# Interleaved high and low activation rows, at fixed offsets modulo 256 bytes, and a 256 / 288 split of the 544 columns

## The chip, the cores and the metric

The kernel runs on one core of a Trainium2 chip. The metric is the time of one execution on the device, in microseconds (us). A difference of about 0.2% is what a measurement of this kernel can tell from no change.

## What is computed

The reference is a two-layer streaming encoder for 512 prompt frames and 32 sample frames of width 1024: in every layer a SwiGLU feed-forward block (hidden size 2816), a recurrent mixer (Mamba-2 and gated linear attention heads in layer 0, HGRN2 heads in layer 1), and a second feed-forward block. Nearly all arithmetic is in dense products of 544 token columns with float32 weights:

```python
def swiglu(x, w_gu, w_down):
    gate, up = jnp.split(x @ w_gu, 2, axis=-1)
    return (jax.nn.silu(gate) * up) @ w_down

for l in range(DEPTH):
    h = h + 0.5 * swiglu(rms_norm(h, p['norm_ffn1'][l]), p['ffn1_w_gu'][l], p['ffn1_w_down'][l])
    u = rms_norm(h, p['norm_mix'][l])
    ...
    h = h + m
    h = h + 0.5 * swiglu(rms_norm(h, p['norm_ffn2'][l]), p['ffn2_w_gu'][l], p['ffn2_w_down'][l])
y = rms_norm(h, p['norm_final'])
```

## The kernel before

Activations lie transposed: 128 features on the partitions, the T = 544 tokens along the free dimension, one "row" of 544 float32 numbers (2176 bytes) for each of KT = 8 groups of 128 features. Each float32 operand is split into a high part (rounded to the type float32r, which TensorE multiplies in one pass) and a low part (the remainder), and a product is made of three: high weight times high row, high weight times low row, low weight times high row.

There are two kinds of dense work on TensorE.

- Plain rows (`row_products`, L2500 to L2516). A unit is one block of 128 output features; it runs over k = 8 (or 6, 4, 7) input rows r and adds all into one line of the PSUM tensor PD. The 544 columns don't fit one PSUM bank of 512, so each product is cut at FRONT = 288 into a front of 288 columns and a rest of 256. One row is six matmuls of 128x128 weights, each with its own weight load.
- Products of the feed-forward up-projections (`product`, L2605 to L2619), a 2x2 block scheme with seven products p1 to p7 for a hidden tile. Each is 4 rows q of three matmuls (L2617, L2618, L2619) with 272 columns, half of T. Products 1, 2, 3 and 7 read XB, 4, 5 and 6 read XT. p1 and p2 start at column 0 of a row, p3 and p7 at column 272.

The moving operands (what streams through TensorE) are these SBUF tensors: XB (the normed input of a block, 8 rows high and 8 rows low), AB (the gated hidden values, rows of the down-projections), YB, GOB and COB (mixer outputs) and XT (sums for the products). In all but XT the eight high rows stand first and the eight low rows behind them, `[2, KT, T]`; x[:, 0, r, :] in `row_products` is the high row r, x[:, 1, r, :] the low one.

Where these tensors start follows from `place`, which lays one after the other, rounded up to 64 bytes. The byte addresses in a partition are: XB 18560, AB and COB 98304, YB and GOB 102528, XT 190464. The weights of plain rows stand in whi and wlo (69760 and on, a block of 512 bytes for each row, so all at 128 modulo 256), the weights of the products in WH and WL (from 133120, all at 0 modulo 256). KW holds the last unit's weights that were loaded early (133120).

The instruction order of each engine is written out by hand. ScalarE rounds weights (whi, L653) and writes high rows (XH L680, AH L763), VectorE makes the low weights (wlo, L1488) and low rows (XL L1526, AL L1658), SyncE issues the weight loads. TensorE waits for them through semaphores at the start of each unit (`lo_ready`, `pair_read`) and, in the first unit over a new operand, at each row.

Of the kernel before, what the change touches and what calls it, by code (L numbers as in the profile page):

```python
# [6 lines left out]
FR = mybir.dt.float32r  # L7
# [5 lines left out]
P = 128  # L13
D = 1024
KT = D // P
TP, TS = 512, 32
T = TP + TS
HT = T // 2
FRONT = 288
REST = T - FRONT  # L20


# [8 lines left out]
KR = 8  # L31
# [18 lines left out]
WHOLE = 3  # L50
# [38 lines left out]
def build(nc, a, o):  # L89
# [3 lines left out]
    with ExitStack() as ctx:  # L93
# [3 lines left out]
        def at(name, shape, offset, dt=F):  # L97
            return nc.alloc_sbuf_tensor_at(name, [P] + list(shape), dt, offset=offset)

        def place(name, shape, where, dt=F):  # L100

            off, n = where[0], 4
            for s in shape:
                n *= s
            where[0] += (n + 63) // 64 * 64
            assert where[0] <= nc.sbuf_usable_end, (name, where[0], nc.sbuf_usable_end)
            return at(name, shape, off, dt)


        w = [(nc.sbuf_base + 63) // 64 * 64]  # L110
        H = place("H", [KT, T], w)
        XB = place("XB", [2, KT, T], w, FR)
        XH, XL = XB[:, 0], XB[:, 1]
        V = at("V", [2, 4, 4 * P], w[0])
        raw = [place(f"raw{s}", [KR, P], w) for s in range(4)]
# [18 lines left out]
        free = w[0]  # L134


        w = [free]
# [5 lines left out]
        SQX = place("SQX", [D], w)  # L143
        WIDE = place("WIDE", [5, P], w)

        w = [free]
        AB = place("AB", [2, 8, T], w, FR)
        AH, AL = AB[:, 0], AB[:, 1]
        late = w[0] + 2 * 7 * 4 * P * 4 - 9 * HT * 4
        WH, WL, WS = {}, {}, {}  # L150
        for b in (1, 0):
# [1 line left out]
            WL[b] = place(f"WL{b}", [7, 4 * P], w, FR)  # L153
            WS[b] = at(f"WS{b}", [4, 4 * P], w[0] - 4 * 4 * P * 4)
        VF = at("VF", [4, 4 * P], late + 9 * HT * 4 - 2 * 7 * 4 * P * 4)
        KW = at("KW", [KT - WHOLE, 2, KR, P], free + 2 * 8 * T * 4, FR)
        assert free + (2 * 8 * T + (KT - WHOLE) * 2 * KR * P) * 4 <= w[0]
        xt_at = w[0]
        XT = place("XT", [2, 4, 3, HT], w, FR)
        tg_at = w[0]  # L160
# [6 lines left out]
        DH = at("DH", [HT], late)  # L167
        XN = at("XN", [HT], late + HT * 4)
        TF = at("TF", [3, HT], late + 2 * HT * 4)
        T3 = at("T3", [4, HT], free + 14 * T * 4)  # L170
        YF = at("YF", [2, T], tg_at)
        yout = at("yout", [NC + 1, D], xt_at)
        assert (NC + 1) * D <= 2 * 4 * 3 * HT
# [1 line left out]
        w = [free]  # L175
# [63 lines left out]
        w = [GM["end"]]  # L239
# [5 lines left out]
        w = [free]  # L245
# [9 lines left out]
        def high_of(u):  # L255

            return KW[:, u - end_unit - WHOLE, 0] if kept(u) else whi[u % 2]

# [11 lines left out]
        def line(b):  # L270

            at0 = 1024 * (b % 2) + 512 - FRONT
            return PDF[:, at0:at0 + T]
# [2225 lines left out]
        def _(pe):  # L2499
            mm = pe.matmul  # L2500

            def row_products(ps, r, x, first, final, before=None):

                out = line(ps)
                front, rest = out[:, 0:FRONT], out[:, FRONT:T]
                hi, lo = high_of(ps)[:, r, :], low_of(ps)[:, r, :]
                if before:
                    before(0)
                mm(front, hi, x[:, 0, r, 0:FRONT], start=first, stop=False)  # L2509
                mm(rest, hi, x[:, 0, r, FRONT:T], start=first, stop=False)  # L2510
                if before:
                    before(1)
                mm(rest, hi, x[:, 1, r, FRONT:T], start=False, stop=False)  # L2513
                mm(front, hi, x[:, 1, r, 0:FRONT], start=False, stop=False)  # L2514
# [89 lines left out]
            def product(s, p):  # L2604

                b, w, out = s % 2, W_OF[p], bank(s, BANK_OF[p])
                if p <= 3:
                    k0, t0 = ((0, 0), (4, 0), (4, HT))[p - 1]
                    moving = XB[:, :, k0:k0 + 4, t0:t0 + HT]
                elif p == 7:  # L2610
                    moving = XB[:, :, 0:4, HT:T]
                else:
# [58 lines left out]
            def ffn(f, e, final=False):  # L2671

                tag = FFNS[f][0]
                if f:
                    run(f"{tag}_up", XB, x_parts(e), lambda: mean_square(e), ORDER if f == 3 else None)
                else:
                    run_rest(f"{tag}_up", XB)
                    pe.wait_ge(S["rs_ready"], 1)
                    for n in range(2):
                        mm(PM[:, n, 0:HT], whi[0][:, 0, :], XH[:, 0, 0:HT], start=True, stop=True)  # L2680
                for g, nf, ss in groups(f):
# [10 lines left out]
                    for s in ss:  # L2692
# [8 lines left out]
                        else:  # L2701
                            unit_rows(u0, 0, 2, nf, AB, before)
                            p3(s)
# [95 lines left out]

            run("ab_small", XB, x_parts(1))  # L2800
            mean_square(1)
# [397 lines left out]
```

## Time and profile before

| | us |
|---|---|
| median of 3 runs | 2326.39 |
| lowest, highest | 2325.65, 2327.73 |
| span of the profiled execution | 2325.5 |

| engine | busy us | share of the span | instructions |
|---|---|---|---|
| PE (matmul) | 2294.0 | 99% | 20579 |
| PEld (weight load) | 2266.2 | 97% | 20579 |
| DVE | 1720.5 | 74% | 2587 |
| ACT | 1143.9 | 49% | 1769 |
| POOL | 14.4 | 1% | 50 |

Matmuls are pipelined: one takes 270 to 310 ns from its start to its end, but the next starts some 120 to 130 ns after it. So the busy time of a matmul is not its price; the price is the distance from its start to the start of the next, which the timeline shows. The timeline's starts are rounded to 0.01 us, so that the length of one row of six matmuls is known to 10 ns from one row, and to 1 or 2 ns from several rows in succession.

### The profile page before, as it was taken

What the parts mean: (1) busy time and instruction counts of PE and PEld (TensorE: products, weight loads), DVE (VectorE), ACT (ScalarE), POOL (GpSimd) and SP (SyncE); (2) the same over time, 40 slices, a digit from 0 to 9 for tenths busy, and PEclk for the clock granted to TensorE, in tenths of its full rate; (3) what the DMA queues carried; (4) which work ended last, traced back from release to release, by engine and by line L of the source; (5) the groups of instructions that cost most, each with busy time, mean ns of one, the idle gap of its engine ahead of it and who ended that gap; (6) DMA issues with size and microseconds to landing.
All of it is one profiled execution on the core that took longest, in us unless ns stands there. A gap on an engine that the chain in (4) does not pass through costs nothing.

```text
span 2325.5 us, 49874 instructions
## 1 busy us (share of the span) xinstructions
PE 2294.0 (99%) x20579; PEld 2266.2 (97%) x20579; DVE 1720.5 (74%) x2587; ACT 1143.9 (49%) x1769; POOL 14.4 (1%) x50
## 2 busy tenths in 40 slices
PE   8999999999999999999999999999999999999998
PEld 8999999999999999999999999999999999999998
DVE  7767876788577567677867767876888867767885
ACT  6434444676354545343445434444677756424453
POOL 1000000000000000000000000000000000000000
PEclk9999999999999999999999999999999999999999
DMA  4323333332422223333323323332222223323331
GB/s 149 105 77 103 94 96 86 94 119 74 121 71 63 76 82 93 98 92 106 95 82 98 111 75 103 95 94 84 70 71 68 69 74 91 96 82 102 88 107 57
DMA packets 397773, 209.92 MB, mean 90 GB/s; under 512 B 11679, under 2 KB 393750, under 8 KB 397558
## 3 DMA queue, kind: packets, MB, share of 16 engines
q1 hardware_dynamic: 392166, 203.17, 30.7%
q10 hardware_dynamic: 5392, 3.72, 0.5%
q8 instruction: 155, 2.54, 0.5%
q14 instruction: 60, 0.49, 0.1%
HBM read 201.41 MB, written 5.45 MB: 89 GB/s over the span
## 4 chain that ended last, share of the span: by engine, by line
PE 83%; DVE 7%; ACT 4%; DVEq 3%; issue 1%; ACTq 1%; DMA 0%; SPq 0%
PE PD L2509 8%; PE PM L2619 8%; PE PM L2617 8%; PE PD L2514 8%; PE PM L2618 8%; PE PD L2515 8%; PE PD L2513 7%; PE PD L2510 7%; PE PD L2516 7%; PE PD L2619 3%; PE PD L2617 3%; PE PD L2618 3%; DVE wlo L1488 1%; DVE c_xl L2199 1%; DVE c_xl L2175 1%
## 5 line engine op out<-in xcount | busy, mean ns | idle before, releaser
L653 ACT ACTIVATE whi<-raw 128x1024 fp32r<-128x1024 f32 (+3 forms) x231 | 229.1, 992 | 356.7 <-PE PD L2516 350.8
L1488 DVE TENSOR_TENSOR wlo<-raw,whi 128x1024 fp32r<-128x1024 f32 (+3 forms) x233 | 267.3, 1147 | 69.3 <-ACT whi L653 47.9
L2509 PE MATMUL PD<-XB,whi 128*128 128x288 f32 x856 | 262.8, 307 | 2.2 <-DVE wlo L1488 2.0
L2514 PE MATMUL PD<-XB,whi 128*128 128x288 f32 x856 | 252.8, 295 | 0.0
L2515 PE MATMUL PD<-XB,wlo 128*128 128x288 f32 x856 | 252.0, 294 | 0.0
L2513 PE MATMUL PD<-XB,whi 128*128 128x256 f32 x856 | 241.9, 283 | 0.3 <-DVE XB L1526 0.3
L2510 PE MATMUL PD<-XB,whi 128*128 128x256 f32 x856 | 240.0, 280 | 0.0
L2516 PE MATMUL PD<-XB,wlo 128*128 128x256 f32 x856 | 238.3, 278 | 0.0
L2619 PE MATMUL PM<-XT,WL 128*128 128x272 f32 x720 | 208.3, 289 | 0.0
L2617 PE MATMUL PM<-XT,WH 128*128 128x272 f32 x720 | 207.6, 288 | 0.0
L2619 PE MATMUL PM<-XB,WL 128*128 128x272 f32 x720 | 207.6, 288 | 0.0
L2617 PE MATMUL PM<-XB,WH 128*128 128x272 f32 x720 | 207.5, 288 | 0.0
L2618 PE MATMUL PM<-XT,WH 128*128 128x272 f32 x720 | 207.1, 288 | 0.0
L2618 PE MATMUL PM<-XB,WH 128*128 128x272 f32 x720 | 207.0, 287 | 0.0
L2509 PE MATMUL PD<-AB,whi 128*128 128x288 f32 x664 | 196.9, 297 | 0.0
L2514 PE MATMUL PD<-AB,whi 128*128 128x288 f32 x664 | 196.4, 296 | 0.0
L2515 PE MATMUL PD<-AB,wlo 128*128 128x288 f32 x664 | 194.6, 293 | 0.0
L2513 PE MATMUL PD<-AB,whi 128*128 128x256 f32 x664 | 188.7, 284 | 0.0
L2510 PE MATMUL PD<-AB,whi 128*128 128x256 f32 x664 | 186.4, 281 | 0.0
L2516 PE MATMUL PD<-AB,wlo 128*128 128x256 f32 x664 | 185.1, 279 | 0.0
L2509 PEld LDWEIGHTS PD<-XB,whi 128*128 128x128 f32 x856 | 161.1, 188 | 5.7 <-issue 2.8
L2515 PEld LDWEIGHTS PD<-XB,wlo 128*128 128x128 f32 x856 | 162.1, 189 | 0.0
(519 smaller groups left out, 6683.7 us busy)
## 6 DMA issues: line engine op xcount, KB each, us to landing
raw<-in_ffn_w_down SPq DMA_DIRECT2D x64, 512.0 KB, 3.8
V<-in_ffn_w_gu SPq DMA_DIRECT2D x60, 512.0 KB, 3.9
V<-in_ffn_w_gu SPq DMA_DIRECT2D x120, 256.0 KB, 4.5
raw<-in_ab_w_in SPq DMA_DIRECT2D x44, 512.0 KB, 3.9
raw<-in_ffn_w_gu SPq DMA_DIRECT2D x32, 512.0 KB, 3.8
raw<-in_c_w_in SPq DMA_DIRECT2D x32, 512.0 KB, 4.0
raw<-in_ffn_w_down SPq DMA_DIRECT2D x32, 384.0 KB, 3.3
VF<-in_ffn_w_gu SPq DMA_DIRECT2D x12, 512.0 KB, 4.6
```

Of the source, the lines that this page charges most:

```text
L653: A(high_of(ps)[:, 0:k, :], raw[ps % 4][:, 0:k, :], ACT.Copy).then_inc(S["hi_ready"], 1)
L1488: TT(low_of(u)[:, 0:k, :], raw[u % 4][:, 0:k, :], high_of(u)[:, 0:k, :].bitcast(F), ALU.subtract).then_inc(S["lo_ready"], 1)
L2175: TT(xn[:, :, 0, :], mid, bn[:, :, 0, :], ALU.subtract)
L2509: mm(front, hi, x[:, 0, r, 0:FRONT], start=first, stop=False)
L2510: mm(rest, hi, x[:, 0, r, FRONT:T], start=first, stop=False)
L2513: mm(rest, hi, x[:, 1, r, FRONT:T], start=False, stop=False)
L2514: mm(front, hi, x[:, 1, r, 0:FRONT], start=False, stop=False)
L2515: mm(front, lo, x[:, 0, r, 0:FRONT], start=False, stop=final)
L2516: return mm(rest, lo, x[:, 0, r, FRONT:T], start=False, stop=final)
L2617: mm(out, hi, moving[:, 0, q, :], start=q == 0 and opens, stop=False, skip_group_check=not opens)
L2618: mm(out, hi, moving[:, 1, q, :], start=False, stop=False, skip_group_check=not opens)
L2619: last = mm(out, lo, moving[:, 0, q, :], start=False, stop=q == 3, skip_group_check=not opens)
```

## The change

The split moves from 288 / 256 to 256 / 288 columns. XB and AB are laid out as `[KT, 2, T]`: the low row of r stands right behind the high row of r. `rearrange` gives all users the old index order, so no other line of XB or AB changes. AB starts 128 bytes later (98432), and 128 bytes are left free behind it, so WH, WL, XT and what follows move by 256 bytes and keep their offset modulo 256, while KW moves by 128. YB, GOB, COB and XT keep their layout.

```diff
@@ -16,7 +16,7 @@
-FRONT = 288
+FRONT = 256
@@ -109,7 +109,7 @@
-        XB = place("XB", [2, KT, T], w, FR)
+        XB = place("XB", [KT, 2, T], w, FR).rearrange("p k s t -> p s k t")
         XH, XL = XB[:, 0], XB[:, 1]
@@ -143,9 +143,11 @@
-        w = [free]
-        AB = place("AB", [2, 8, T], w, FR)
+        ab_at = free + 128
+        w = [ab_at]
+        AB = place("AB", [8, 2, T], w, FR).rearrange("p k s t -> p s k t")
         AH, AL = AB[:, 0], AB[:, 1]
+        w[0] += 128
         late = w[0] + 2 * 7 * 4 * P * 4 - 9 * HT * 4
@@ -153,8 +155,8 @@
-        KW = at("KW", [KT - WHOLE, 2, KR, P], free + 2 * 8 * T * 4, FR)
-        assert free + (2 * 8 * T + (KT - WHOLE) * 2 * KR * P) * 4 <= w[0]
+        KW = at("KW", [KT - WHOLE, 2, KR, P], ab_at + 2 * 8 * T * 4, FR)
+        assert ab_at + (2 * 8 * T + (KT - WHOLE) * 2 * KR * P) * 4 <= w[0]
@@ -167,7 +169,7 @@
-        T3 = at("T3", [4, HT], free + 14 * T * 4)
+        T3 = at("T3", [4, HT], ab_at + 14 * T * 4)
```

Every engine has the same instructions in the same order (16040 rows on PE, 2412 on DVE, 1611 on ACT, 524 on SP); on PE the widths of the plain matmuls differ. One row of a down-projection unit (moving operand AB, high weights whi, low weights wlo, both numbered) and the first matmul of the next, on PE, before:

```order
L2509 MATMUL PD<-AB,whi_57 128x288
L2510 MATMUL PD<-AB,whi_57 128x256
L2513 MATMUL PD<-AB,whi_57 128x256
L2514 MATMUL PD<-AB,whi_57 128x288
L2515 MATMUL PD<-AB,wlo_59 128x288
L2516 MATMUL PD<-AB,wlo_59 128x256
L2509 MATMUL PD<-AB,whi_56 128x288
```

The same place in the changed kernel, where the source lines have moved by two:

```order
L2511 MATMUL PD<-AB,whi_57 128x256
L2512 MATMUL PD<-AB,whi_57 128x288
L2515 MATMUL PD<-AB,whi_57 128x288
L2516 MATMUL PD<-AB,whi_57 128x256
L2517 MATMUL PD<-AB,wlo_59 128x256
L2518 MATMUL PD<-AB,wlo_59 128x288
L2511 MATMUL PD<-AB,whi_56 128x256
```

Nothing moved; each 288 has become a 256 and each 256 a 288, three of each in a row as before.

The start of each of the six reads, modulo 256 bytes, follows from the addresses. A row is 2176 bytes, 8.5 times 256, and eight rows are 68 times 256, so before, a high row and its low row started alike, and every other r started at the other offset. A front of 288 columns is 4.5 times 256 bytes, one of 256 columns 4 times.

| matmul of the row | before, row start at 0 | before, row start at 128 | after, XB and AB, every row |
|---|---|---|---|
| high weight, high row, front | 0 (288 columns) | 128 (288) | 128 (256 columns) |
| high weight, high row, rest | 128 (256) | 0 (256) | 128 (288) |
| high weight, low row, rest | 128 (256) | 0 (256) | 0 (288) |
| high weight, low row, front | 0 (288) | 128 (288) | 0 (256) |
| low weight, high row, front | 0 (288) | 128 (288) | 128 (256) |
| low weight, high row, rest | 128 (256) | 0 (256) | 128 (288) |

Before, rows with an even r start at 0 in AB and COB and at 128 in XB, YB and GOB; rows with an odd r the other way round.

## Rows read from the trace of the kernel before

**Rows 1.** The page: span, busy time and share by engine, part 2, part 4.

```profile
span 2325.5 us, 49874 instructions
...
PE 2294.0 (99%) x20579; PEld 2266.2 (97%) x20579; DVE 1720.5 (74%) x2587; ACT 1143.9 (49%) x1769; POOL 14.4 (1%) x50
...
PEclk9999999999999999999999999999999999999999
...
PE 83%; DVE 7%; ACT 4%; DVEq 3%; issue 1%; ACTq 1%; DMA 0%; SPq 0%
```

**Rows 2.** Costliest groups (line engine op, shapes, count, busy us, mean ns, idle before).

```profile
L2509 PE MATMUL PD<-XB,whi 128*128 128x288 f32 x856 | 262.8, 307 | 2.2 <-DVE wlo L1488 2.0
...
L2510 PE MATMUL PD<-XB,whi 128*128 128x256 f32 x856 | 240.0, 280 | 0.0
...
L2617 PE MATMUL PM<-XB,WH 128*128 128x272 f32 x720 | 207.5, 288 | 0.0
...
L2509 PE MATMUL PD<-AB,whi 128*128 128x288 f32 x664 | 196.9, 297 | 0.0
...
L2617 PE MATMUL PD<-XB,WH 128*128 128x272 f32 x432 | 124.6, 288 | 0.0
```

**Rows 3.** Timeline of PE, us 959 to 964: start, length, instruction; rows 2 to 7.

```profile
959.31 0.29 PE L2619 MATMUL PM<-XT,WL 128*128 128x272 f32 x1
959.44 0.29 PE L2617 MATMUL PM<-XT,WH 128*128 128x272 f32 x1
959.57 0.28 PE L2618 MATMUL PM<-XT,WH 128*128 128x272 f32 x1
959.69 0.29 PE L2619 MATMUL PM<-XT,WL 128*128 128x272 f32 x1
959.82 0.29 PE L2509 MATMUL PD<-AB,whi 128*128 128x288 f32 x1
959.95 0.28 PE L2510 MATMUL PD<-AB,whi 128*128 128x256 f32 x1
960.06 0.28 PE L2513 MATMUL PD<-AB,whi 128*128 128x256 f32 x1
...
960.56 0.30 PE L2509 MATMUL PD<-AB,whi 128*128 128x288 f32 x1
960.70 0.28 PE L2510 MATMUL PD<-AB,whi 128*128 128x256 f32 x1
960.82 0.28 PE L2513 MATMUL PD<-AB,whi 128*128 128x256 f32 x1
...
961.32 0.30 PE L2509 MATMUL PD<-AB,whi 128*128 128x288 f32 x1
...
964.34 0.30 PE L2509 MATMUL PD<-AB,whi 128*128 128x288 f32 x1
```

**Rows 4.** The same view, GOB units; the first line is row 0, the second row 2 of unit 1.

```profile
818.09 0.29 PE L2509 MATMUL PD<-GOB,whi 128*128 128x288 f32 x1
...
826.03 0.30 PE L2509 MATMUL PD<-GOB,whi 128*128 128x288 f32 x1
...
826.79 0.30 PE L2509 MATMUL PD<-GOB,whi 128*128 128x288 f32 x1
...
827.54 0.30 PE L2509 MATMUL PD<-GOB,whi 128*128 128x288 f32 x1
```

**Rows 5.** The same view, XB units: eight rows in succession.

```profile
1687.85 0.30 PE L2509 MATMUL PD<-XB,whi 128*128 128x288 f32 x1
...
1693.87 0.30 PE L2509 MATMUL PD<-XB,whi 128*128 128x288 f32 x1
```

**Rows 6.** The same view, another stretch of XB units.

```profile
1960.68 0.29 PE L2509 MATMUL PD<-XB,whi 128*128 128x288 f32 x1
...
1961.42 0.29 PE L2509 MATMUL PD<-XB,whi 128*128 128x288 f32 x1
...
1963.67 0.29 PE L2509 MATMUL PD<-XB,whi 128*128 128x288 f32 x1
```

## The prediction

> **What bounds the kernel now.** I read the page first: TensorE is busy for 2294.0 of 2325.5 us, the chain of work that ended last runs through it for 83%, and its granted clock is full in all forty slices [rows 1]. Some 31 us of the span are left in which it is idle, and the largest group of idle time in front of a plain row is 2.2 us, for low weights [rows 2]. So the time is the number of matmuls times the distance between the starts of two, and no other engine's work is worth a microsecond here. The matmul durations (280 to 307 ns, [rows 2]) are pipelined and say nothing of that distance; it has to be taken from the timeline.
>
> There, one row of a down-projection starts at 959.82, the next at 960.56, the next at 961.32 [rows 3]: 0.74 and 0.76 us. The six rows to 964.34 take 4.52 us [rows 3], so a pair takes 1.507 us and a row 753 ns on average. Both rows of a pair are the same six matmuls of the same widths, back to back, with no wait shown between them. To split the 1.507 us I lean on the repeats: the starts at 10 ns fit a short row of about 747 and a long one of about 760 ns, in turns.
>
> What differs between the two is the address. These lines follow the last products of a group, so they are rows 2 and 3 of their unit (rows 0 and 1 stand before the products in `ffn`, L2702 to L2705). In AB an even row starts at 0 modulo 256 and is the short one. In GOB an even row starts at 128: row 2 of its second unit starts at 826.03, row 3 at 826.79, row 4 at 827.54 [rows 4], so that the even row takes 0.76 and the odd one 0.75. The parity is reversed, and the offset is not: the row that starts at 0 is short in both. I take it that **the offset modulo 256 bytes sets the distance**, at 13 ns in a row.
>
> Within the row, the step that shows it is that from L2510 to L2513, both with 256 columns. It is 0.11 us in the short row (959.95 to 960.06) and 0.12 in the long one (960.70 to 960.82) [rows 3]. In the short row these 256 wide reads start at 128, in the long one at 0. The 288 wide L2509 takes 0.13 or 0.14 either way [rows 3]. So my reading is: the narrow matmuls, three in each row, are some 4 ns slower each when they start at 0 (13 ns over three), and the wide ones hardly mind. whi and wlo all start at 128, so it may be the agreement of the moving read with the weight load beside it that helps; for XB and AB under the change this comes to the same thing.
>
> XB has the same two kinds of rows, eight of them in 1693.87 - 1687.85 = 6.02 us, 752.5 ns each [rows 5], but stretches of it run a little faster: four rows in 1963.67 - 1960.68 = 2.99 us, 747.5 ns each, with the short one at 0.74 [rows 6]. The same addresses thus have more than one steady rhythm. I take 751 as XB's mean, nearer to rows 5, since more of the stretches I looked at are of that kind.
>
> **The change part by part.** Three of its parts have one answer and cost nothing by themselves. The writes of high and low rows by ScalarE and VectorE keep their sizes and their count, with TensorE behind them 99% busy. T3, TF, WS and the others only move. The queues of SyncE, ScalarE, VectorE and GpSimd keep their order, no wait is added, and nothing new is in front of any instruction. What hides all of these is TensorE's work. If that cover were gone it would show as idle time in front of L2511, where now 2.2 us stand for XB [rows 2].
>
> *Plain rows over XB and AB.* There are 856 and 664 of them [rows 2]. In the new layout every row has the same six offsets, so all rows should take the same time, in place of two kinds in turns. The three narrow reads are at 128, 0 and 128 (before: all three at 128 in a short row, all three at 0 in a long one). By the price above, one of three at the bad offset gives 747 + 4 = 751 ns. Against that, four of the six successions from one matmul to the next keep their offset now, and three did before, in both kinds; and where they are kept at 128 the step was the shortest of all, 0.11 us. The unknown is the change from the high row at 128 to the low row at 0, in wide reads, which no row shows. Bounds from both sides: not better than the fastest kind of row seen, 0.74 us [rows 6], for which I take 743 ns (a pair there takes 1.495 us, and the other row 0.75), not worse than the slowest, 760 ns [rows 3]. I take **747 ns**, the short kind: the new row has the same three widths of each kind in a cycle, most reads at the good offset, and the rhythms seen are few and apart, so a row with one bad narrow read of three should fall into the nearer one. That gives:
>
> - AB: 664 x (753 - 747) = 4.0 us less.
> - XB: 856 x (751 - 747) = 3.4 us less.
>
> Both ends: at 743 ns it would be 664 x 10 + 856 x 8 = 13.5 us less, at 760 ns 664 x 7 + 856 x 9 = 12.4 us more.
>
> *Plain rows over YB, GOB, COB.* They keep two kinds of row. With the cut at 256 columns front and rest start alike, so that a row at 128 has all its reads at 128 and a row at 0 all at 0. The narrow reads are good in one kind and bad in the other, as before. There are fewer than 200 such rows; at 3 ns each way it is 0.6 us at most, and I take 0.
>
> *Products.* Widths don't change, offsets do, in those that read XB: 720 + 432 = 1152 rows q of three matmuls [rows 2]. Before, high and low row were at the same offset (0 or 128, 64 or 192 from column 272 on). Now the high row is at 128 or 192 and the low one 128 bytes off, so that of three successions one is kept in place of two. XT, whose addresses keep their offset, shows what such steps are: 0.13, 0.13, 0.12, 0.13 us [rows 3], 125 ns on average, with single steps off by a few ns. I see no row by which the new order is dearer or cheaper and take 0. The bounds are one step of three by 3 ns either way: 1152 x 3 = 3.5 us.
>
> *Sum.* 7.4 us less on TensorE. Some XB rows stand in stretches where TensorE waits a little for low weights or for the mixer's vector work; 31 idle us of 2325 are 1.3%, and a row that gets shorter there only waits longer. I take 5% off: 7.0 us. The profiled execution (2325.5 us) would take 2318.5; the median of the runs stands 0.9 us above the profiled span, so the forecast is 2326.4 - 7.0 = **2319.4 us**.
>
> A rule of the Trainium skill speaks against any effect. The page "TensorE: Matmul & The Clock Gate", section "Back-to-back issue gap", gives the distance of two warm matmuls as N / 2.4 GHz + 2.5 ns, with no address in it, and the same page says that the next weights' load doesn't take read bandwidth from the running matmul. An estimate by that page is 3 x 122.5 + 3 x 109.2 = 695 ns for a row, before and after, and a change of 0. The trace disagrees on the size, with 747 and 760 ns, and on the address, since equal widths differ by 13 ns.
>
> **The rivals.**
>
> *No change.* The two kinds of row could come from a state that TensorE carries from one row to the next, or the gain at narrow reads could be eaten by the wide change from 128 to 0 and by the products. Then a row stays at 751 to 753, or products cost their 3.5 us: 2322 to 2328 us, 2326 if nothing moves. For it speaks that XB shows two rhythms at the same addresses [rows 5, 6], so the address isn't all. Against it: the parity goes with the offset in AB and in GOB [rows 3, 4].
>
> *Slower.* The change of offset between high and low row of one matmul pair comes twice in each row (high weight from 128 to 0, then back to 128 with the low weight) and could throw every row into the long kind. Price: 12.4 us on 1520 rows, less 5%: 2326.4 + 11.8 = 2338 us. It decides from the point at which these two changes cost more than 4 ns each over the steps now, since 751 + 9 is 760. For it: the one narrow read at 0 now comes right between the two changes. Against it: in a short row the offset changes three times (before L2510, after L2513, before L2516), and the row is short all the same.
>
> *Twice the gain.* Rows fall to 743 ns, as in the fast stretches of XB [rows 6]: 13.5 us less, 2313 us. For it: four kept successions, and the stretch shows that TensorE can do so at these widths. Against it: the fastest rhythm was seen with all narrow reads at the good offset.
>
> **How the numbers follow.** The forecast has 0.45, twice the gain 0.12, no change 0.27, slower 0.16. The first two give faster by more than 0.2% (4.7 us, about what a measurement of this kernel can tell from no change), so faster 0.57, same 0.27, slower 0.16. The range is to leave out 2 in 10: it drops the slow case at 2338 and the edge of the fastest, and reaches from 2311 (743 ns with products 1.5 us better) to 2331 (no change with the products 3.5 us worse, and 1 us for the two ends of a measurement).
>
> **What would show it.** In the timeline after, all rows of AB and XB should be equally long, 0.75, 0.74, 0.75 us between the starts of L2511, eight rows in 5.98 us. If they still come in turns, the address is not the cause. If all are at 0.76, the slow rival holds. The step after a narrow read at 128 should be 0.11 to 0.12, after the one at 0 0.12. Eight rows of three product matmuls should stay at 3.0 us. The count and order of everything, the granted clock and the 31 us of idle time should be as they were. The prediction is wrong if the rows have a length of their own outside 743 to 760, or if the products, 1152 rows of three that I priced at nothing, move by more than 3 ns each.

## The result: 5 us slower

| | before | after |
|---|---|---|
| median of 16 runs, us | 2326.59 | 2331.64 |
| lowest, highest | 2325.01, 2327.94 | 2329.82, 2334.14 |
| span of the profiled execution | 2325.5 | 2330.1 |

The ratio after / before is 1.0023, with a 95% interval of 1.0016 to 1.0029. The forecast was 2319.4 us, the range 2311 to 2331: wrong in its sign, and 0.6 us outside the range.

The page of the changed kernel: span, busy time by engine, granted clock, and the shares of the chain that ended last. They answer to [rows 1].

```profile
span 2330.1 us, 49874 instructions
...
PE 2302.4 (99%) x20579; PEld 2275.8 (98%) x20579; DVE 1721.2 (74%) x2587; ACT 1143.9 (49%) x1769; POOL 13.7 (1%) x50
...
PEclk9999999999999999999999999999999999999999
...
PE 83%; DVE 7%; ACT 4%; DVEq 3%; issue 1%; ACTq 1%; POOL 0%; POOLq 0%
```

Counts and clock are as before, and the chain runs through the same engines; the groups of plain and of product rows have the same idle time in front of them as in [rows 2], within 0.3 us. TensorE's idle time as a whole isn't quite what it was: 2330.1 - 2302.4 = 27.7 us, against 31.5 before. 2.6 us of this difference lie in the first 24 us of the span (TensorE busy for 18.9 us there before, 21.5 after). That is no gain: the dense rows that follow start 0.7 us later than before.

```profile
L2511 PE MATMUL PD<-XB,whi 128*128 128x256 f32 x856 | 251.0, 293 | 1.9 <-DVE wlo L1490 1.8
...
L2619 PE MATMUL PM<-XB,WH 128*128 128x272 f32 x720 | 207.7, 288 | 0.0
```

So the 4.6 us of the two spans have to be looked for in the distances. Adding up the distances from each matmul's start to the next over the whole of both traces gives:

| TensorE time, us | before | after | difference |
|---|---|---|---|
| plain rows over XB | 666.5 | 668.5 | +2.0 |
| plain rows over AB | 500.8 | 503.0 | +2.2 |
| plain rows over YB, GOB, COB | 150.1 | 150.6 | +0.5 |
| products over XB | 434.2 | 434.6 | +0.4 |
| products over XT | 325.9 | 325.8 | -0.1 |
| everything else | 238.2 | 237.8 | -0.4 |

Nearly everything is in the plain rows, where the forecast had put it, with the other sign. In XB the sum hides some of it. Ordinary steps (under 160 ns) are 125.06 ns on average before and 126.09 after, 5.2 us over some 5000 of them. Against that, the steps of 160 ns and more sum to 42.3 us before (145 of them) and 37.5 after (132). 1.6 us of this is a stretch at half the granted clock, near 1946 us in the trace of before, and another 1.6 are shorter breaks (the last 1.6 of the 4.8 are the 13 steps that are ordinary ones now). In AB, where almost nothing is waited for (nine steps of 160 ns and more in either trace, 1.9 us), the ordinary steps go from 125.51 to 126.07 ns, which is its 2.2 us.

The timeline of the changed kernel in a down-projection shows how (start, length, instruction; one whole row, then the first matmul of each following row; it answers to [rows 3]).

```profile
973.11 0.29 PE L2511 MATMUL PD<-AB,whi 128*128 128x256 f32 x1
973.24 0.29 PE L2512 MATMUL PD<-AB,whi 128*128 128x288 f32 x1
973.37 0.30 PE L2515 MATMUL PD<-AB,whi 128*128 128x288 f32 x1
973.50 0.28 PE L2516 MATMUL PD<-AB,whi 128*128 128x256 f32 x1
973.63 0.28 PE L2517 MATMUL PD<-AB,wlo 128*128 128x256 f32 x1
973.75 0.29 PE L2518 MATMUL PD<-AB,wlo 128*128 128x288 f32 x1
973.88 0.28 PE L2511 MATMUL PD<-AB,whi 128*128 128x256 f32 x1
...
974.64 0.28 PE L2511 MATMUL PD<-AB,whi 128*128 128x256 f32 x1
...
975.38 0.28 PE L2511 MATMUL PD<-AB,whi 128*128 128x256 f32 x1
...
976.14 0.29 PE L2511 MATMUL PD<-AB,whi 128*128 128x256 f32 x1
...
988.24 0.29 PE L2511 MATMUL PD<-AB,whi 128*128 128x256 f32 x1
```

The rows take 0.77, 0.76, 0.74 and 0.76 us, and then it begins again. From 976.14 to 988.24 there are 16 rows in 12.10 us, 756 ns each. The unrounded starts give the cycle as 769, 757, 748 and 753 ns. **Yet all these rows have identical widths and identical offsets**, and the cycle of four is not tied to the row number. The mean over all rows of AB went from 753.0 to 756.5 ns and of XB from 751.1 to 756.3.

### The profile page after: what moved, and what is told of

Same layout as the page of the kernel before. It is cut to its first block, busy times and chain, and to the rows that moved or that the text cites. A ratio compares the mean times of both kernels' runs of the same rounds, so it can differ in the third digit from the quotient of the medians.

```text
span 2330.1 us, 49874 instructions
## 1 busy us (share of the span) xinstructions
PE 2302.4 (99%) x20579; PEld 2275.8 (98%) x20579; DVE 1721.2 (74%) x2587; ACT 1143.9 (49%) x1769; POOL 13.7 (1%) x50
## 4 chain that ended last, share of the span: by engine, by line
PE 83%; DVE 7%; ACT 4%; DVEq 3%; issue 1%; ACTq 1%; POOL 0%; POOLq 0%
PE PM L2621 8%; PE PM L2619 8%; PE PD L2512 8%; PE PM L2620 8%; PE PD L2518 8%; PE PD L2515 8%; PE PD L2511 7%; PE PD L2516 7%; PE PD L2517 7%; PE PD L2619 3%; PE PD L2621 3%; PE PD L2620 3%; DVE wlo L1490 1%; DVE c_xl L2201 1%; DVE c_xl L2177 1%
## 5 line engine op out<-in xcount | busy, mean ns | idle before, releaser
L2512 PE MATMUL PD<-XB,whi 128*128 128x288 f32 x856 | 253.3, 296 | 0.0
L2515 PE MATMUL PD<-XB,whi 128*128 128x288 f32 x856 | 252.7, 295 | 0.3 <-DVE XB L1528 0.3
L2511 PE MATMUL PD<-XB,whi 128*128 128x256 f32 x856 | 251.0, 293 | 1.9 <-DVE wlo L1490 1.8
L2516 PE MATMUL PD<-XB,whi 128*128 128x256 f32 x856 | 240.8, 281 | 0.0
L2516 PE MATMUL PD<-AB,whi 128*128 128x256 f32 x664 | 186.9, 281 | 0.0
L2511 PEld LDWEIGHTS PD<-XB,whi 128*128 128x128 f32 x856 | 161.5, 189 | 5.5 <-issue 2.8
L2512 PEld LDWEIGHTS PD<-XB,whi 128*128 128x128 f32 x856 | 161.1, 188 | 0.5
```

## The experiments

Two theories stood at first. **The sequence**: how long a row takes depends on the rows before it, and only the mean over the whole repeating stream means anything. **The offsets**: every kind of row has its own length, mine were wrong for some. Later runs ask which part of the sequence costs the 3 ns. In the results, "mean row" is the mean distance between row starts over a whole trace (from the unrounded starts). Times are medians, ratios are against the kernel before on the same chip, with the 95% interval; where a kernel ran only once, no ratio is given. The trace is always that of one execution.

### One part of the change alone

**split_only**: the cut alone, with the old layout.

```diff
-FRONT = 288
+FRONT = 256
```

> Only the cut moves, from 288 / 256 to 256 / 288 columns; XB and AB keep the old layout. Theory A (a plain row's length goes with the agreement of its reads' offset with that of the weights, both modulo 256 bytes): as in YB, GOB and COB of the changed kernel, rows at 128 take 744 ns and rows at 0 take 764 ns in XB and AB too, 1507 ns a pair as before, so the time stays at 2326 us, within 1. Theory B (the loss is in the cut itself, whose rows then cycle with a mean of 756 ns): 2331 us.

2328.43 against 2326.85 us, 1.0011 [1.0001, 1.0020]; span 2326.5. In the old layout with this cut, a row lies with all six reads at 0 or all at 128. The first matmuls of five rows of a down-projection unit:

```profile
961.42 0.28 PE L2509 MATMUL PD<-AB,whi 128*128 128x256 f32 x1
...
962.18 0.27 PE L2509 MATMUL PD<-AB,whi 128*128 128x256 f32 x1
...
962.93 0.28 PE L2509 MATMUL PD<-AB,whi 128*128 128x256 f32 x1
...
963.69 0.27 PE L2509 MATMUL PD<-AB,whi 128*128 128x256 f32 x1
...
964.43 0.28 PE L2509 MATMUL PD<-AB,whi 128*128 128x256 f32 x1
```

Rows at 0 take 763 ns, rows at 128 take 744: further apart than before (760, 747), but the pair is 1507 ns as it was [rows 3]. What the one kind gains, the other pays. The medians differ by 1.6 us, more than was expected. In XB the faster rhythm of [rows 6] is gone: its mean row is 753.9, 2.8 ns more than before, 2.4 us over 856 rows, which is enough for that difference.

**layout_only**: the layout alone, with the cut at 288.

```diff
-        XB = place("XB", [2, KT, T], w, FR)
+        XB = place("XB", [KT, 2, T], w, FR).rearrange("p k s t -> p s k t")
-        AB = place("AB", [2, 8, T], w, FR)
+        AB = place("AB", [8, 2, T], w, FR).rearrange("p k s t -> p s k t")
```

(AB, KW, WH and what follows are placed as in the changed kernel.)

> Only the layout of XB and AB moves (high and low row side by side, AB at 128); the cut stays at 288 / 256. Theory A (the low row at the other offset than the high row makes the loss): 2331 us, a mean of 756 ns for rows of XB and AB, and 753 for YB, GOB, COB as before. Theory B (the cut makes the loss): 2326 us and pairs of 1507 ns.

2329.03 against 2326.85 us, 1.0009 [0.9999, 1.0019]; span 2327.0. Mean row 753.3 (AB) and 752.7 (XB), all rows nearly alike. Neither theory had expected this. So the layout makes rows alike, as meant, and the equal row is the old *average*, not the short kind. In AB neither part alone costs anything (501.1 us for the cut, 501.0 for the layout, 500.8 before), while both together cost 2.2 us: there the loss is an interaction. In XB half of the 5.2 ns a row comes with the cut, as the fast rhythm goes (751.1 to 753.9), and the other half only with both (756.3).

### Whose offset is it?

**split_weights0**: the cut at 256 and the weights whi, wlo at 0 instead of 128 modulo 256.

```diff
-FRONT = 288
+FRONT = 256
+        w[0] += 128
         whi = [place(f"whi{s}", [KR, P], w, FR) for s in range(2)]
         wlo = [place(f"wlo{s}", [KR, P], w, FR) for s in range(2)]
+        w[0] += 128
```

> Cut at 256 in the old layout, and the weights of plain rows (whi, wlo) moved by 128 bytes to offset 0 modulo 256. Theory A (offset relative to the weights decides): the kinds of row change places, 744 ns for rows at 0 and 764 ns for rows at 128; time 2326 us. Theory B (the moving read's own offset decides): 744 ns for rows at 128 and 764 ns for rows at 0 as in the kernel with the cut alone; time 2326 us.

2329.63 us, 1.0010 [1.0000, 1.0019]; span 2327.7. The first of these rows is row 2, the same number as the first one shown of split_only:

```profile
961.21 0.28 PE L2511 MATMUL PD<-AB,whi 128*128 128x256 f32 x1
...
961.95 0.28 PE L2511 MATMUL PD<-AB,whi 128*128 128x256 f32 x1
...
962.72 0.27 PE L2511 MATMUL PD<-AB,whi 128*128 128x256 f32 x1
...
963.46 0.28 PE L2511 MATMUL PD<-AB,whi 128*128 128x256 f32 x1
```

The kinds have changed places: now the row at 0 takes 744 ns and the one at 128 takes 763, and so they do over the whole of XB, AB and GOB. **What picks the short row, in this layout, is the moving read's offset relative to that of the weights.** The activations weren't touched. The sum of a pair again didn't move.

**weights_match**: the weight blocks are stored by the parity of r, so that each row's weights stand at the same offset as its moving row; AB and COB start 128 bytes later, the cut is at 256. Every read then agrees with its weights.

```diff
+        half = 4 * (KR // 2 * P) + 32
+        whi = [at(f"whi{s}", [2, half], w[0] + s * 2048, FR) for s in range(2)]
...
+            return x[:, r % 2, r // 2 * P:r // 2 * P + P] if len(x.shape) == 3 and x.shape[-1] != P else x[:, r, :]
...
-                hi, lo = high_of(ps)[:, r, :], low_of(ps)[:, r, :]
+                hi, lo = wrow(high_of(ps), r), wrow(low_of(ps), r)
```

> Cut at 256, old layout of rows, AB and COB moved to 128, and the weights of odd rows placed 128 bytes off those of even rows, so that in every row weights and moving reads have the same offset modulo 256. Theory A (relative offset): every plain row takes 744 ns, 8 ns less than now over 1707 rows, some 12 us less on TensorE, 2315 us. Theory B (the moving read's own offset): rows at 128 take 744 and rows at 0 764 ns, time 2326 us. A third way, a cycle over several rows as in the changed kernel since the offset changes from row to row: a mean near 753, 2326 us.

2325.21 against 2326.85 us, 0.9995 [0.9986, 1.0005]; span 2323.4. All rows are at 748 to 752. **weights_match_again**, the same kernel once more, with 11 runs:

> The kernel weights_match once more, with more rounds, since its row length was 750 ns everywhere (3.3 ns less than 753.3): 1707 rows less 3 ns, some 3 to 5 us less on TensorE, against 1 to 2 us measured. If the gain is real: 2322 to 2325 us against 2326.5, a ratio of 0.9985 to 0.9995. If it was noise: 1.000.

2325.41 against 2326.38 us, 0.9996 [0.9987, 1.0005]; span 2323.7, mean row 750. In both, the row is 3 ns shorter than the 753 of most streams, and in both the time can't be told from that of the kernel before, so a gain in time isn't established. It is surely not the 744 ns a row, and 12 us, that were expected if every row was of "the good kind".

**match_288**: the same placing with the cut at 288, so that the front agrees with the weights and the rest doesn't.

```diff
-FRONT = 256
+FRONT = 288
```

> Weights of odd rows 128 bytes off those of even rows, in step with the rows, with the cut at 288: in every row the fronts are at the weights' offset and the rests 128 off. Theory A: all rows of the long kind, 760 ns, 10 us more than the kernel before (2337 us). Theory B (the steps come from the shift between successive reads, in which weights and rows now move together): a length of its own near 750 ns, 2324 us.

2327.00 against 2326.2 us, 1.0004 [0.9995, 1.0014]; span 2325.2. Rows take 753 and 747 in turns in most places, and in others there are rows of 757 among them; the mean is 751.8 (AB), 752.0 (XB). The 760 that a price by kind asks for isn't there.

**opposite_288**: each weight block 128 bytes off its row's start, cut at 288; the rest agrees and the front doesn't, in every row.

```diff
+        w[0] += 128
         half = 4 * (KR // 2 * P) + 32
...
```

> The same cut at 288, with the weights 128 bytes off the row start in every row: fronts 128 off, rests at the weights' offset, which was the short kind. Theory A: all rows 747 ns, 1707 rows times 5 ns less, 2318 us. Theory B: near 750 ns as its counterpart, 2323 us.

2328.30 us, 1.0008 [0.9998, 1.0018]; span 2326.7. Timeline, first matmuls of rows in AB:

```profile
966.02 0.29 PE L2528 MATMUL PD<-AB,whi 128*128 128x288 f32 x1
...
966.79 0.29 PE L2528 MATMUL PD<-AB,whi 128*128 128x288 f32 x1
...
967.53 0.29 PE L2528 MATMUL PD<-AB,whi 128*128 128x288 f32 x1
...
968.30 0.29 PE L2528 MATMUL PD<-AB,whi 128*128 128x288 f32 x1
...
969.04 0.29 PE L2528 MATMUL PD<-AB,whi 128*128 128x288 f32 x1
```

Rows of 766 and 741 ns in turns, though each has the same offsets relative to its weights. In XB either parity can be the short one. This speaks for the sequence and against any price by kind: it is the largest difference seen between two neighbours, and their sum is 1507 again.

### Does a row have a length of its own?

**even_rows_288** and **even_rows_256** read row r - r % 2 in place of r, with the cut at 288 and at 256. They leave the odd rows of the moving operand out of the result; the work is the same. Now all rows of a tensor stand at one offset.

```diff
-                mm(front, hi, x[:, 0, r, 0:FRONT], start=first, stop=False)
-                mm(rest, hi, x[:, 0, r, FRONT:T], start=first, stop=False)
+                mm(front, hi, x[:, 0, r - r % 2, 0:FRONT], start=first, stop=False)
+                mm(rest, hi, x[:, 0, r - r % 2, FRONT:T], start=first, stop=False)
...
```

> The kernel before with every plain row's six matmuls reading the row below it when r is odd (r - r % 2), so that the moving reads of all rows of one tensor have one offset: 128 in XB, YB, GOB, the weights' own, and 0 in AB and COB. The weights, widths and waits stay; the output isn't the reference's. Theory A (each row's length is set by its own offset relative to the weights): 760 ns for all rows of XB and 747 ns for all of AB. Theory B (a row's length depends on what came before, and the two kinds only exist in turns): both tensors get about the pair's mean of 753 ns.

One run: 2327.34 us, beside 2326.2 for before; span 2325.6. AB's rows, all at 0 and all of the kind that took 747 in turns with 760, take 750, 752 and 758 in a cycle of three, mean 753.3. XB's, all at 128, take 760, 741 and 753 in a cycle of three, mean 751.3.

> The same with the cut at 256 columns: every read of XB at the weights' offset, every read of AB 128 bytes off it; the output isn't the reference's. Theory A: 744 ns for all XB rows, 764 ns for all AB rows. Theory B: both near 753 ns.

One run: 2326.41 us; span 2324.7. XB's rows, with each read at the weights' offset, the kind that took 744, take 753.2 each; AB's, with none there, the kind that took 763, take 751 and 756, 753.4 on average. **Two kinds that differ by 19 ns in turns are equal when each stands alone.** No length belongs to a kind of row. With this the theory that an offset gives a row its length has fallen. In these two kernels each even row is also read twice in succession, and what that does by itself wasn't measured; opposite_288, which reads every row once, says the same.

### Which part of the changed row makes the cycle?

**after_low_at_high**: the changed kernel, with the two matmuls of the low row reading the high row. It leaves the low rows' products out of the result; the offsets no longer change within a row.

```diff
-                mm(rest, hi, x[:, 1, r, FRONT:T], start=False, stop=False)
-                mm(front, hi, x[:, 1, r, 0:FRONT], start=False, stop=False)
+                mm(rest, hi, x[:, 0, r, FRONT:T], start=False, stop=False)
+                mm(front, hi, x[:, 0, r, 0:FRONT], start=False, stop=False)
```

> The changed kernel with the plain rows' two matmuls over the low row reading the high row of the same r, so that all six reads of a row of XB and AB stand at 128, the weights' offset; the output isn't the reference's. Theory C (the loss of the change is its alternation between a high row at 128 and a low row at 0 inside each row, which puts TensorE into a cycle of four rows of 769, 757, 748 and 753 ns): every row 753 ns as with even rows alone, 3.2 ns less over 1520 rows, 5 us less than the changed kernel, 2326.5 us. Theory D (the loss comes with the new layout or places of other tensors): stays at 2331 us.

```profile
975.21 0.28 PE L2511 MATMUL PD<-AB,whi 128*128 128x256 f32 x1
...
975.96 0.28 PE L2511 MATMUL PD<-AB,whi 128*128 128x256 f32 x1
...
976.72 0.28 PE L2511 MATMUL PD<-AB,whi 128*128 128x256 f32 x1
...
981.24 0.28 PE L2511 MATMUL PD<-AB,whi 128*128 128x256 f32 x1
```

The cycle of four is gone: eight rows in 6.03 us, mean 753.4 (AB) and 753.3 (XB), and AB's rows cost 501.0 us again. So the low row at the other offset makes the 3 ns, given the cut at 256. The total moved less than that: 2329.92 against 2326.38 us, 1.0011 [1.0002, 1.0021], span 2329.3. Some 1.9 us of the 3.5 that are left can come from XB, whose 856 rows take 753.3 ns and not the 751.1 of the kernel before; the rest isn't explained. The profiled execution also has more time at half the granted clock than that of the changed kernel: from 1895 to 1900 us the mean granted clock is 0.66 (1.00 in the changed kernel), and from 8 to 16 us, near the start, it is 0.57 (also 1.00 there). For the next two kernels too it is the rows, not the totals, that show the loss gone: the medians stay 2.8 and 4.0 us above the kernel before.

**after_reordered**: the changed kernel, with the low weights' matmuls before the low row's, so that the offset changes twice in a row at other places (the high weights are used again at the end).

```diff
+                mm(rest, lo, x[:, 0, r, FRONT:T], start=False, stop=False)
+                mm(front, lo, x[:, 0, r, 0:FRONT], start=False, stop=False)
...
-                mm(rest, hi, x[:, 1, r, FRONT:T], start=False, stop=False)
-                mm(front, hi, x[:, 1, r, 0:FRONT], start=False, stop=False)
-                mm(front, lo, x[:, 0, r, 0:FRONT], start=False, stop=final)
-                return mm(rest, lo, x[:, 0, r, FRONT:T], start=False, stop=final)
+                mm(front, hi, x[:, 1, r, 0:FRONT], start=False, stop=final)
+                return mm(rest, hi, x[:, 1, r, FRONT:T], start=False, stop=final)
```

> The changed kernel with the low weights' two matmuls ahead of the low row's: high row four times at 128, then low row twice at 0; the widths stay 256, 288, 288, 256, 256, 288. As many changes of offset in a row as in the changed kernel (two), at another width: between 256 and 256, and between 288 and the next row's 256, in place of 288 to 288 and 256 to 256. Theory C in its narrow form (the change from 128 to 0 between two wide matmuls makes the long cycle): a mean of 750 to 753 ns, 2322 to 2327 us. In its wide form (any row with four reads at the weights' offset and two off it averages 756): 2331 us.

2329.22 against 2326.38 us, 1.0009 [0.9999, 1.0018]; span 2328.9, mean row 753.4 and 753.0. The same offsets in another order give the common 753.

**after_weights0**: the changed kernel, with whi and wlo at 0 modulo 256 (the two added lines of split_weights0).

> The changed kernel with whi and wlo moved to offset 0, so that the high rows are 128 bytes off the weights and the low rows agree with them. Theory C with relative offsets in which only the changes count: the same cycle, mean 756 ns, 2331 us. If agreement of high row and weights counts as well: another mean, up to 3 ns a row (5 us) away on either side.

2330.33 us, 1.0014 [1.0004, 1.0023]; span 2327.0, mean row 753.3 (AB) and 753.5 (XB). With the other relation to the weights the 3 ns are gone as well.

**match_reordered** and **before_reordered**: the same reordering with the weights placed as in weights_match, and in the kernel before.

> The kernel weights_match with the low weights' two matmuls ahead of the low row's; offsets all equal inside a row as there, since high and low row, high and low weights of a row agree. If only offsets and widths count, the order of operands changes nothing: 750 ns a row, 2325.3 us. If it counts which tile is read twice in succession, another mean.

2324.26 against 2326.55 us, 0.9991 [0.9982, 1.0001]; span 2322.4, mean row 750.

> The kernel before with the same reordering and nothing else; every address sequence stays, since high and low row have the same offset. If only offsets and widths count: 747 and 760 ns in turns, 1507 a pair, and 2326 us.

One run: 2325.85 us; span 2324.1; 747 and 760 in turns in AB, mean 753, and 751.3 in XB, as before. The 64 rows over GOB run in the faster rhythm of [rows 6] here, 751 and 743, where before they took 760 and 747. Apart from that the order of the operands alone moves nothing.

### Widths in turns

In the kernel before, widths come as 288, 256, 256, 288, 288, 256: twice in a row two equal ones follow each other. Two lines swapped make them strictly alternate.

**after_widths** and **after_widths_again**: that swap in the changed kernel.

```diff
-                mm(rest, hi, x[:, 1, r, FRONT:T], start=False, stop=False)
                 mm(front, hi, x[:, 1, r, 0:FRONT], start=False, stop=False)
+                mm(rest, hi, x[:, 1, r, FRONT:T], start=False, stop=False)
```

> The changed kernel with front and rest strictly in turns (256, 288, 256, 288, 256, 288 columns), so that the offsets stay 128, 128, 0, 0, 128, 128 but both changes of offset come between a wide matmul and a narrow one. Narrow theory C (the loss needs the change between two wide matmuls and between two narrow ones): rows of 750 to 753 ns, 2326 us. Wide theory C (two changes of offset against fixed weights, wherever they stand, give 756): 2331 us.

2323.96 against 2326.55 us, 0.9990 [0.9980, 1.0000]; span 2322.2. That is below both expectations, so the same kernel ran again.

> after_widths once more with more rounds, since it was the fastest so far (0.9990 of the kernel before, interval 0.998 to 1.0). If real: 2324 us, ratio 0.9985 to 0.9995, rows of XB and AB in two steady lengths, 747 and 753 ns.

2323.37 against 2326.14 us, 0.9987 [0.9978, 0.9997]; span 2323.2; mean row 747.3 (XB) and 749.9 (AB). From the timeline of this one, first matmuls of rows of one unit and the next:

```profile
1068.06 0.28 PE L2511 MATMUL PD<-AB,whi 128*128 128x256 f32 x1
...
1070.32 0.28 PE L2511 MATMUL PD<-AB,whi 128*128 128x256 f32 x1
...
1071.24 0.28 PE L2511 MATMUL PD<-AB,whi 128*128 128x256 f32 x1
...
1074.98 0.28 PE L2511 MATMUL PD<-AB,whi 128*128 128x256 f32 x1
```

Three rows take 753 ns each up to 1070.32; then one takes 0.92, and behind it five take 748 each. The instructions are the same on both sides. One stream has two steady lengths, and a short break switches from one to the other.

**before_widths**: the same swap in the kernel before.

> The kernel before with front and rest in turns (288, 256, 288, 256, 288, 256) and nothing else. If turns of widths make the gain of after_widths by themselves: rows of 747 to 750 ns, 2323 to 2325 us. If they need the change's offsets (four reads at the weights' offset, two off it): 753 ns, 2326.5 us.

**2316.87 against 2326.14 us** (five runs; lowest 2316.19, highest 2319.29), ratio 0.9957 [0.9944, 0.9971]. Three lines of its page: the span, the busy times, and the group of XB rows:

```profile
span 2317.6 us, 49874 instructions
...
PE 2283.3 (99%) x20579; PEld 2253.7 (97%) x20579; DVE 1721.1 (74%) x2587; ACT 1144.0 (49%) x1769; POOL 13.3 (1%) x50
...
L2509 PE MATMUL PD<-XB,whi 128*128 128x288 f32 x856 | 259.9, 304 | 2.4 <-DVE wlo L1488 2.0
```

And its timeline, one row and the start of the next:

```profile
972.20 0.29 PE L2509 MATMUL PD<-AB,whi 128*128 128x288 f32 x1
972.33 0.28 PE L2510 MATMUL PD<-AB,whi 128*128 128x256 f32 x1
972.45 0.29 PE L2513 MATMUL PD<-AB,whi 128*128 128x288 f32 x1
972.58 0.28 PE L2514 MATMUL PD<-AB,whi 128*128 128x256 f32 x1
972.69 0.29 PE L2515 MATMUL PD<-AB,wlo 128*128 128x288 f32 x1
972.82 0.28 PE L2516 MATMUL PD<-AB,wlo 128*128 128x256 f32 x1
972.94 0.29 PE L2509 MATMUL PD<-AB,whi 128*128 128x288 f32 x1
...
987.81 0.29 PE L2509 MATMUL PD<-AB,whi 128*128 128x288 f32 x1
```

From 972.94 to 987.81 there are 20 rows in 14.87 us, 743.5 ns each, in both kinds of offset (742.4 and 744.3 in turns; over the whole trace the mean is 744.0 in AB and 744.6 in XB). Both expectations were too high. TensorE's plain rows cost 664.1 (XB) and 495.1 us (AB), which is 2.4 and 5.7 us less than before. This is faster than both kernels: 9.3 us below the kernel before, 14.8 below the changed one (whose runs were on another chip).

**match_widths**: the swap with the weights and the cut of weights_match.

> weights_match with front and rest in turns (256, 288, ...). If the two gains add (3.3 ns a row from weights in step, up to 6 ns from turns): 745 ns or less, 2318 to 2322 us. If turns only help where offsets change inside a row: 750 ns, 2325 us.

2325.76 against 2326.14 us, 0.9998 [0.9989, 1.0007]; span 2323.9; rows of 748 and 752, mean 750. The two helpful-looking edits don't add: of the three layouts in which widths were put in turns, only the old one gives 744.

## Why the prediction was wrong

| stream of plain rows (cut first) | lengths seen, ns | mean |
|---|---|---|
| before, 288 | 747, 760 | 753 |
| split_only, 256 | 744, 763 | 753.5 |
| layout_only, 288 | 753 | 753 |
| opposite_288 | 741, 766 | 753.5 |
| even_rows_256 | 753 (XB); 751 to 756 (AB) | 753 |
| after_low_at_high, 256 | 753 | 753 |
| weights_match, 256 | 748 to 752 | 750 |
| changed kernel, 256 | 769, 757, 748, 753 | 756.5 |
| after_widths, 256 | 747 or 753 | 747 to 750 |
| before_widths, 288 | 742 to 745 | 744 |

- **What bounds the kernel**: right. TensorE's distances carry the difference, 4.2 of 4.6 us in the plain rows of XB and AB, and no other engine's work has a part that shows. One reading was too strong: "its granted clock is full in all forty slices". A 9 on the page of the profile stands for 90% or more, and the trace of before has two stretches of 3.4 us at half the granted clock in its middle, near 583 and 1945 us.
- **"The offset modulo 256 bytes sets the distance"**: this is the step that failed. The rows it rested on [rows 3, 4] were read rightly, and the parity does go with the offset. But two rows that always follow each other give two numbers that can't be told apart: a long one may be the repayment of the short one before it. even_rows_256 separates them (753 and 753 for what had been 744 and 763). The table shows that the sum of a pair stays at 1507 while its halves lie anywhere from 741 and 766 to 753 and 753.
- **"The narrow matmuls, three in each row, are some 4 ns slower each when they start at 0"**: falls with it, also as a term of the sum: no run shows a price of 4 ns for a narrow read. The step after L2516, with 256 columns and at 0 in every row of the changed kernel, takes 123, 122, 112 and 119 ns in its cycle of four.
- **"whi and wlo all start at 128, so it may be the agreement"**: right as a side remark, and shown by split_weights0. "For XB and AB under the change this comes to the same thing" was wrong: after_weights0 keeps the changed activations, moves only the weights, and is 3 ns a row faster.
- **747 ns for the new row**: it measured 756.5 (AB) and 756.3 (XB). The term 664 x (753 - 747) = 4.0 us less became 664 x 3.5 = 2.3 us more, and 856 x (751 - 747) = 3.4 us less became 856 x 5.2 = 4.4 us more by the mean row. These 6.7 us less the 5% for breaks would be 6.4, and 4.2 showed in the sums: 1.6 us of the rest is the half-clock stretch that the trace of before had in XB and that of after had not, the other 0.6 lies within the breaks. "The rhythms seen are few and apart" named the right picture and then picked a rhythm with no ground for it. The likeliest guess for a row of equal neighbours was the mean of the pair, 753.
- **The rival "no change"** gave the right reason ("a state that TensorE carries from one row to the next") and had 0.27. The row that spoke for it, two rhythms at the same addresses [rows 5, 6], should have weighed more: one such row refutes a length by address.
- **The rival "slower"** had the right sign, and the right place: the high row at 128 and the low row at 0 are what makes the cycle (after_low_at_high). Its price, every row at 760 (7 ns more in AB, 9 in XB), was about twice the 3.5 and 5.2 ns measured; one row in four is at 769, and the others are at 748 to 757.
- **Products, YB, GOB, COB, writes at 0**: right, within 0.5 us for each term. (The four XT steps of [rows 3] come to 127.5 ns, not the 125 of the text; over the whole trace it is 125.7.) The 31 us of idle time, which were to stay, became 27.7. The YB, GOB and COB rows, with their old layout and the new cut, became 744 and 763 in turns, as in split_only.
- **The rule of the Trainium skill**: by the page "TensorE: Matmul & The Clock Gate", section "Back-to-back issue gap", a row would be 695 ns whatever its addresses. What the prediction left out is that the section gives this formula for a matmul by itself, and for a stream of matmuls with weight loads 81 ns at 128 columns and 131 ns at 512; an estimate on a straight line between these is 98 to 102 ns for 256 to 288 columns. The trace disagrees with both: it has 124.0 to 126.1 ns a matmul, which is 744 to 756.5 ns for the same three wide and three narrow ones. Whether a weight load takes read bandwidth from the running matmul was not tested by any run, but moving the weights alone made the changed kernel's mean row 3 ns shorter (after_weights0).

**What stays open.** The runs show which edits remove the 3 ns of the changed kernel: the low row at the high row's offset, the cut back at 288, the weights at 0, the low weights' matmuls first, the widths in turns. Each of the five alone does it, so the cycle belongs to the whole sequence and there is no single costly instruction to point at. What carries the state from one row to the next, and why the common mean is 753 and the exceptions are 744, 750 and 756.5, no run here tells. One thing moves with the cut that the description of the change doesn't name: `line` starts a unit's output at column 512 - FRONT of its PSUM bank, so that the front's output starts at column 224 with the cut at 288 and at 256 with the cut at 256. No run parts this from the widths and the reads' offsets. It isn't enough for the loss by itself, as after_low_at_high, after_reordered and after_weights0 have it too and run at 753, but it may be one of its conditions. Nor was it tried whether widths in turns help the products, whose widths are all 272.

## What to carry to other kernels

When rows come in turns, long and short, first ask what the pair costs; a gain computed from making all rows like the short one is worth nothing until one stream of only short rows has been seen. In a stream bound by TensorE's issue distance, the order of widths is a knob worth one cheap run: two swapped lines gave 0.4% here, and most of the gain wasn't there with the other two layouts (after_widths, match_widths), so each combination has to be measured. Judge by the mean over a long stretch (16 rows or more), never by single steps.

## What the runs showed of the hardware

- The distance between two matmuls with own weight loads and equal widths isn't fixed. For a row of 3 x 288 + 3 x 256 columns it averaged 124.0, 125.0, 125.5 or 126.1 ns (before_widths, weights_match, layout_only, the changed kernel), by the order of widths and by the offsets modulo 256 bytes of moving operand and weights, at a granted clock of 0.997 to 0.998 over the span, that is at 2.4 GHz nearly throughout. All offsets were moved by 128 bytes. That 256 bytes are the period is borne out by rows r and r + 2, which stand 17 times 256 bytes apart and take the same length (split_only).
- Streams of identical rows settle into cycles of one, two, three or four rows (layout_only; even_rows_256 in AB; even_rows_288; the changed kernel), and a short break can switch between two of them (after_widths_again).
- A wait of TensorE for VectorE, 2.12 us long, was followed by a stretch at half the granted clock (1.2 GHz). It needn't be: in even_rows_256 the same wait took 2.13 us, and the granted clock stayed at 1.00. The line is that of the changed kernel's first matmul after it, and the window is of its TensorE: mean granted clock 0.66 over five microseconds, that is 3.4 us at 0.5.

```profile
584.16 1.12 PE L2900 MATMUL PM<-SQY,ones 128*128 128x512 f32 x2 [2.12 <-DVEq L2013]
```

```profile
584.00:589.00 5.00, 4.84 (x21) 4.36 (x22) 3.07 (x5) 1.64 (x3) 0.00 (x0) 0.66 0.35 105
```

Executions differ in how many such stretches they have (none to two in the middle, here near 583, 1893 and 1945 us), and each costs about 1.7 us (half of 3.4): the rows over YB take 52.4 to 52.6 us in the traces that have a whole stretch in them and 50.7 to 51.0 in those that have none. That is a third of the effect that was looked for, and it is the reason why only the sums of distances, not two medians, could place the 3 ns a row.
